# A hybrid decoder layer on one core: the pooling map folded into the output weight, weight parts loaded by another queue, and three edits of order

## The chip, the cores and the metric

The kernel runs on one core of a Trainium2 chip. The metric is the device time of one execution in microseconds (us), as the median of several runs.

## What is computed

One decoder layer over 2048 tokens of width 1024, in fp32. The parts that matter here:

```python
z = rmsnorm(h, g_attn_norm) @ w_in          # q (512), k (128), v (128), u (512)
a = sliding_window_sink_attention(q, k, v, sinks, rel_bias)   # window 128, blocks of 128
# u in 4 groups of 128 channels; group g: trailing mean over 2/4/8/16 tokens, minus the token
pooled = stack((cs - lag) / cnt - u)                          # (S, 4, 128)
m = einsum('bsgc,gcd->bsgd', pooled, w_pool) * pool_scale
h = h + concatenate([a, m]) @ w_out
h = h + (silu(hn @ w_gate) * (hn @ w_up)) @ w_down            # hn = rmsnorm(h, g_ffn_norm)
h = h + sigmoid(rmsnorm(h, g_ple_norm) @ w_ple_gate) * (p @ w_ple_proj)
```

The map of the pooled values, the scale and the lower half of w_out are linear and follow each other: group g of m times its rows of w_out equals pooled_g times (w_pool_g · diag(pool_scale_g) · w_out rows of g).

## The kernel before

**Numbers in two parts.** Every operand of a matmul is split into a high part (an ACT copy that rounds to fp32r, at 1042 for weights) and a low part (DVE's difference, at 1554), and a product is three matmuls: high·high, low·high, high·low. So each panel of weights (128 x 1024, 512 KB) is loaded into raw, split, and used by 24 matmuls of 512 columns.

**Stages.** Tokens go in four tiles of 512. For each tile t there is a z section (10 panels, 20 halves of 12 matmuls: the projections to q, k, v, u) and an output section (8 panels, 16 halves). The order is z0, z1, o0, z2, o1, z3, o2, o3. The attention of a tile is cut into 19 steps that are hosted between halves of later sections (table `HOST`): tile 0 densely in z1, tile 1 in o0 and z2, tile 2 in o1 and z3, tile 3 in o2 and o3. A step's work is spread over all engines: logits, transposes and attention products on TensorE; softmax input, reciprocal, low parts and sums on DVE; exponentials, scaling and copies on ACT; pooling sums and the sinks on GpSimd. After that come, for each half of the tokens, the feed-forward section (seven products by Strassen-like sums), the down projection, and two gate sections (`ple_section`), the first of which is mixed with the norm of the second pair of tiles.

**The pooled values.** GpSimd builds window sums (`sum_level`), DVE forms the mean minus the token (`pool_mean`), ACT and GpSimd split it (`pooled_hi`, `pool_rest`). Then `pool_y` on TensorE maps it with w_pool (2484 to 2486), ACT scales and rounds the result (`pool_y_hi`, 1148) and DVE takes the low part (`pool_y_rest`, 1772), back into the tile's mix buffers. That is done 16 times, at the halves in `POOL_Z`, `POOL_O2` and `POOL_O3`; output sections and, for tile 3, attention products wait for the low part (`y_lo`).

**Queues.** The order of each engine is written out by hand, in program order, with semaphores. SP issues x, raw panels, bias, h, the feed-forward inputs and their stores. Weights of panels 10 to 27 are split once, stored in two parts (`w_split`), and for panels 28 to 71 the parts are fetched again by GpSimd (`load_parts`, 858) into three slots. A pair waits for `panel_used >= i - 2`, that is until the panel three places earlier has been used. In an output section t < 2, eight chunks of x of tile t+2 pass through four stage slots (`load_chunk`, 553): chunk k is scaled by ACT at half 2+k (`CHUNK_AT`) and squared in the half behind it; chunks 4 to 7 reuse the slots. The staging of k and q of the next tile (1087, 1096) is on ACT's list at half 9, and its first logits at half 11 (2392).

**Start.** ACT issues three gains and waits for all (48), then scales x (1056), splits the first panel, and issues eight constants. **Gate.** In the first section of a pair (2677 and on), TensorE turns the added squares (`turn_squares`, 2351) behind the first pair of chunks and the reciprocal roots (2357) behind the second; ACT's four late squares (1049) and GpSimd's sums (824) come just ahead.

The wait for a weight panel differs by its place, which is what the edits of queue touch:

```python
def panel_ready(i):
    if has_parts(i):
        pe.wait_ge(parts_landed[parts_slot(i)], 32 * ((i - SPLIT_END) // SLOTS_W + 1))
    else:
        pe.wait_ge(lo_done, split_of(i) + 1)
```

## Time and profile before

| | |
|---|---|
| median of 3 runs | 2050.03 us |
| lowest and highest | 2048.8 and 2052.91 us |
| the profiled execution | 2053.4 us, span 2051.5 us |
| mean granted clock of TensorE | 0.998 |
| DMA | 292.09 MB, mean 142 GB/s |

PE is TensorE's matmuls, PEld its weight loads (they overlap PE), DVE VectorE, ACT ScalarE, POOL GpSimd, SP the sync engine; a q behind a name is the engine's sequencer. "Idle before it" names what ended an engine's wait; "issue" is time in which it waited for nothing that the profile shows. The granted clock is a share of 2.4 GHz: 0.5 is 1.2 GHz. A landing is counted from the issue. Matmuls overlap at their ends, so that their distance, not their duration, is what one costs.

### The profile page before, as it was taken

What the parts mean: (1) busy time and instruction counts of PE and PEld (TensorE: products, weight loads), DVE (VectorE), ACT (ScalarE), POOL (GpSimd) and SP (SyncE); (2) the same over time, 40 slices, a digit from 0 to 9 for tenths busy, and PEclk for the clock granted to TensorE, in tenths of its full rate; (3) what the DMA queues carried; (4) which work ended last, traced back from release to release, by engine and by line L of the source; (5) the groups of instructions that cost most, each with busy time, mean ns of one, the idle gap of its engine ahead of it and who ended that gap; (6) DMA issues with size and microseconds to landing.
All of it is one profiled execution on the core that took longest, in us unless ns stands there. A gap on an engine that the chain in (4) does not pass through costs nothing.

```text
span 2051.5 us, 26122 instructions
## 1 busy us (share of the span) xinstructions
PE 2011.2 (98%) x9546; PEld 1663.4 (81%) x9546; DVE 1372.9 (67%) x1920; ACT 899.7 (44%) x1460; POOL 406.5 (20%) x508
## 2 busy tenths in 40 slices
PE   8999999999999999999999999999999999999998
PEld 6887878877788888888888878788888888888877
DVE  4696674767696665655888765966566566987663
ACT  4575754657433333333333543533333333334542
POOL 4454644645410000000000220000000000001310
PEclk9999999999999999999999999999999999999999
DMA  7757566364934223225825128432322328352143
GB/s 193 201 180 245 188 236 219 130 236 131 347 127 130 81 72 103 72 72 171 307 62 165 36 72 223 143 119 67 96 85 72 100 79 292 130 159 78 42 134 103
DMA packets 197387, 292.09 MB, mean 142 GB/s; under 512 B 16139, under 2 KB 118452, under 8 KB 195980
## 3 DMA queue, kind: packets, MB, share of 16 engines
q1 hardware_dynamic: 172672, 212.97, 34.1%
q0 software_dynamic: 22176, 76.96, 10.8%
q8 instruction: 76, 1.25, 0.3%
q10 hardware_dynamic: 2412, 0.50, 0.1%
q14 instruction: 51, 0.42, 0.1%
HBM read 223.25 MB, written 67.51 MB: 142 GB/s over the span
## 4 chain that ended last, share of the span: by engine, by line
PE 84%; DVE 6%; DMA 3%; issue 3%; ACT 2%; POOL 1%; SPq 0%; ACTq 0%; DVEq 0%; POOLq 0%
PE bank L2623 13%; PE bank L2627 13%; PE bank L2625 13%; PE bank L2660 7%; PE bank L2661 7%; PE bank L2662 7%; PE bank L2323 4%; PE bank L2325 4%; PE bank L2324 4%; PE bank L2299 2%; PE bank L2301 2%; PE bank L2300 2%; DMA w_parts<-w_split 1%; PE bank L2392 1%; DVE w_lo L1554 1%
## 5 line engine op out<-in xcount | busy, mean ns | idle before, releaser
L2623 PE MATMUL bank<-a_hi,ring_hi 128*128 128x512 f32 x1232 | 479.7, 389 | 1.0 <-DVE ring_lo L1917 0.7
L2627 PE MATMUL bank<-a_hi,ring_lo 128*128 128x512 f32 x1232 | 479.3, 389 | 0.0
L2625 PE MATMUL bank<-a_lo,ring_hi 128*128 128x512 f32 x1232 | 479.3, 389 | 0.0
L2623 PEld LDWEIGHTS bank<-a_hi,ring_hi 128*128 128x128 f32 x1232 | 231.3, 188 | 49.9 <-DVE ring_lo L1917 1.4
L2625 PEld LDWEIGHTS bank<-a_lo,ring_hi 128*128 128x128 f32 x1232 | 231.3, 188 | 48.0
L2627 PEld LDWEIGHTS bank<-a_hi,ring_lo 128*128 128x128 f32 x1232 | 231.3, 188 | 47.8
L2660 PE MATMUL bank<-d_hi 128*128 128x512 f32 x616 | 239.8, 389 | 0.0
L2662 PE MATMUL bank<-d_hi,d_lo 128*128 128x512 f32 x616 | 239.7, 389 | 0.0
L2661 PE MATMUL bank<-d_lo,d_hi 128*128 128x512 f32 x616 | 239.6, 389 | 0.0
L1376 ACT ACTIVATE d_hi<-keep 128x1024 fp32r<-128x1024 f32 x132 | 139.8, 1061 | 201.9 <-PE bank L2662 184.9
L975 POOL DMA_DIRECT2D hidden_T<-hid x88 | 47.6, 541 | 770.4 <-DVE hid L1953 750.7
L2047 DVE TENSOR_TENSOR d_lo<-keep,d_hi 128x1024 fp32r<-128x1024 f32 x132 | 163.9, 1244 | 52.9 <-ACT d_hi L1376 52.8
L1289 ACT ACTIVATE ring_hi<-raws 128x1024 fp32r<-128x1024 f32 x80 | 84.7, 1058 | 218.5 <-PE bank L2627 208.0
L1917 DVE TENSOR_TENSOR ring_lo<-raws,ring_hi 128x1024 fp32r<-128x1024 f32 x80 | 98.7, 1234 | 99.1 <-ACT ring_hi L1289 99.1
L1554 DVE TENSOR_TENSOR w_lo<-raw,w_hi 128x1024 fp32r<-128x1024 f32 x68 | 87.5, 1287 | 100.4 <-ACT w_hi L1042 100.0
L2662 PEld LDWEIGHTS bank<-d_hi,d_lo 128*128 128x128 f32 x616 | 115.6, 188 | 24.2
L2660 PEld LDWEIGHTS bank<-d_hi 128*128 128x128 f32 x616 | 115.6, 188 | 23.9
L2661 PEld LDWEIGHTS bank<-d_lo,d_hi 128*128 128x128 f32 x616 | 115.6, 188 | 23.8
L824 POOL TENSOR_TENSOR acc<-acc,sq 128x512 f32<-128x512 f32 x72 | 110.8, 1539 | 117.8 <-ACT sq L1049 112.8
L1917 DVE TENSOR_TENSOR ring_lo<-t,ring_hi 128x1024 fp32r<-128x1024 f32 x63 | 77.2, 1226 | 66.7 <-ACT ring_hi L1289 66.7
L1042 ACT ACTIVATE w_hi<-raw 128x1024 fp32r<-128x1024 f32 x68 | 71.8, 1055 | 111.5 <-PE bank L2325 63.3
L1289 ACT ACTIVATE ring_hi<-t 128x1024 fp32r<-128x1024 f32 x63 | 66.5, 1056 | 108.2 <-DVE t L1903 108.2
(258 smaller groups left out, 3879.9 us busy)
## 6 DMA issues: line engine op xcount, KB each, us to landing
w_parts<-w_split POOLq DMA_DIRECT2D x88, 512.0 KB, 4.8
hidden_T<-hid POOLq DMA_DIRECT2D x88, 256.0 KB, 2.3
raws<-in_w_gate SPq DMA_DIRECT2D x80, 256.0 KB, 4.7
raws<-in_w_up SPq DMA_DIRECT2D x80, 256.0 KB, 5.1
keep<-hidden_T SPq DMA_DIRECT2D x66, 256.0 KB, 3.8
raw<-in_w_ple_gate SPq DMA_DIRECT2D x64, 256.0 KB, 4.2
keep<-in_w_down SPq DMA_DIRECT2D x44, 256.0 KB, 4.4
other<-hidden_T SPq DMA_DIRECT2D x44, 256.0 KB, 6.8
```

What stands on the lines that cost most here:

```text
L824: nc.gpsimd.tensor_tensor(into[:, :], slots[:, 0, :] if j == 1 else into[:, :], slots[:, j % 2, :], ALU.add).then_inc(acc_done, 1)
L1289: nc.scalar.activation(ring_of(half, m)[0][:, :, :], ring_source(half, m), ACT.Copy).then_inc(ring_hi_done, 1)
L1376: nc.scalar.activation(d_hi[s % SLOTS][:, :, :], down_pair(s)[0], ACT.Copy).then_inc(d_hi_done, 1)
L1554: nc.vector.tensor_tensor(panel_lo(i), panel_raw(i), panel_hi(i).bitcast(F32), ALU.subtract).then_inc(lo_done, 1)
L1917: nc.vector.tensor_tensor(lo[:, :, :], ring_source(half, m), hi[:, :, :].bitcast(F32), ALU.subtract).then_inc(ring_lo_done, 1)
L2047: nc.vector.tensor_tensor(d_lo[s % SLOTS][:, :, :], down_pair(s)[0], d_hi[s % SLOTS][:, :, :].bitcast(F32), ALU.subtract).then_inc(d_lo_do ...
L2623: mm(dst[:, :], wh[:, g, cols], a_hi[o][:, k, :], start=fresh and k == 0, stop=False, skip_group_check=True)
L2625: mm(dst[:, :], wh[:, g, cols], a_lo[o][:, k, :], start=False, stop=False, skip_group_check=True)
L2627: ins = mm(dst[:, :], wl[:, g, cols], a_hi[o][:, k, :], start=False, stop=k == 3, skip_group_check=True)
L2660: mm(dst, wh[:, cols], ah, start=fresh and k == 0, stop=False, skip_group_check=True)
L2661: mm(dst, wh[:, cols], al, start=False, stop=False, skip_group_check=True)
L2662: ins = mm(dst, wl[:, cols], ah, start=False, stop=k == FPAIRS - 1, skip_group_check=True)
```

## The change

Five edits in one:

1. **The pooling map goes into the output weight.** During z0 GpSimd loads the four 128-row groups of w_out's lower half (`load_pooled_rows`); ACT and DVE scale and split them (`pooled_rows_hi`, `pooled_rows_lo`); TensorE multiplies each by w_pool (now loaded transposed), 2 x 3 matmuls per group (`mix_rows`); ACT copies the banks (`copy_mixed`), GpSimd stores them to `w_mixed` (`store_mixed`), and the output panels with pooled rows are read from there. `pool_y`, `pool_y_hi` and `pool_y_rest` are gone, the mix buffers keep the pooled values, and their readers wait for `pool_lo`. Three engines wait at half 4 or 5 of z1 for the stores, SP ahead of the first output panel.
2. **Parts by the sync queue.** `load_parts` moves from GpSimd's list to SP's, between the other transfers; the first four chunks of x and h of tile 1 are issued together at the end of z2 instead of behind it, and the loads of feed-forward inputs in o3 change their order.
3. **The start.** Twelve matmuls on zeros (`WARM`) once the memsets are done; a one-element ACT copy, with which the table is loaded first; ACT waits for one gain instead of three; the other two gains and the eight constants are issued by GpSimd.
4. **The gate's turn.** Turning the squares and the roots comes one pair of chunks later, and so do the sums, scalings and splits that hang on them; the split of the fourth panel stands between the late squares.
5. **u behind attention.** In halves that host a step without fresh logits, DVE copies u behind the step instead of ahead.

```diff
-POOL_Z, POOL_Z_COPY = {14: (0,), 16: (1,), 17: (2,), 18: (3,)}, {15: (0,), 17: (1,), 18: (2,), 19: (3,)}
-POOL_O2, POOL_O2_COPY = {9: (0,), 13: (1,), 15: (2,)}, {9: (0,), 13: (1,), 15: (2,)}
-POOL_O3, POOL_O3_COPY = {0: (3,)}, {0: (3,)}
+POOLED_HI_AT, POOLED_LO_AT = {10: 0, 11: 1, 12: 2, 13: 3}, {11: 0, 12: 1, 13: 2, 14: 3}
+POOLED_AT, POOLED_COPY_AT = {13: 0, 14: 1, 15: 2, 16: 3}, {14: 0, 15: 1, 16: 2, 17: 3}
+POOLED_STORE_AT = {16: (0, 1), 17: (2,), 18: (3,)}
+WARM = 12
...
-                return rows(w_out, 2 * r, 2 * r + 2, cols)
+                return rows(w_mixed[:, :], 2 * r - 4, 2 * r - 2, cols)
...
+            def load_parts(i):
...
+                    sp.wait_ge(panel_used, i - SLOTS_W + 1)
+                sp.wait_ge(parts_stored[kept % 2], 32 * (kept // 2 + 1))
+                for part in range(2):
+                    sp.dma_start(w_parts[parts_slot(i)][:, part, :].bitcast(F32), w_split[kept, part]
+                                   ).then_inc(parts_landed[parts_slot(i)], 16)
...
                     load_z(t + 1, c)
+                    if t == 1 and c == 0:
+                        load_parts(Z_AT[2] + 1)
+                    if t:
+                        load_parts(Z_AT[t + 1] + c + 2)
...
+                    if t == 1 and c == 9:
+                        for k in range(4):
+                            load_chunk(3, k)
+                        for b in range(NB):
+                            load_h(1, b)
...
                     load_out(t, c)
-                    if t == 1 and c == 0:
-                        for k in range(4):
-                            load_chunk(3, k)
-                        for b in range(NB):
-                            load_h(1, b)
+                    if t == 0 and c == 7:
+                        load_parts(Z_AT[2])
+                    if t:
+                        load_parts(OUT_AT[t] + c + 2)
                     if t < 2:
                         for k in {3: (4,), 4: (5, 6), 5: (7,)}.get(c, ()):
                             load_chunk(t + 2, k)
...
+            def pooled_rows_hi(g):
+                if g == 0:
+                    act.wait_ge(consts, CONSTS + 16 * NPOOL)
+                nc.scalar.activation(wo_hi[g][:, :], wo_raw[g][:, :], ACT.Copy,
+                                     scale=scale_sb[:, g:g + 1]).then_inc(wp_hi_done, 1)
...
-                    for j in range(4, KC):
-                        square_late(g + 1, j)
+                    square_late(g + 1, 4)
+                    square_late(g + 1, 5)
+                    split(ple + 3)
+                    square_late(g + 1, 6)
+                    square_late(g + 1, 7)
...
-            act.dma_start(gains[:, 1, :], g_ffn).then_inc(gain_landed, 16)
-            act.dma_start(gains[:, 2, :], g_ple).then_inc(gain_landed, 16)
-            act.wait_ge(gain_landed, 48)
+            act.wait_ge(constants_set, 1)
+            nc.scalar.activation(neg_max[:, 0, 0:1], minus_half[:, :], ACT.Copy)
+            act.wait_ge(gain_landed, 16)
...
-            load_constants()
...
+            def mix_rows(g):
+                pe.wait_ge(wp_lo_done, g + 2)
+                if g == 0:
+                    pe.wait_ge(kvcopied, NB)
+                elif g >= 2:
+                    pe.wait_ge(mixed_copied, 2 * g - 2)
+                for e in range(2):
+                    dst, cols = mixed_bank_of(g, e), slice(e * T, (e + 1) * T)
+                    mm(dst[:, :], wp_hi[:, g, :], wo_hi[g][:, cols], start=True, stop=False)
+                    mm(dst[:, :], wp_hi[:, g, :], wo_lo[g][:, cols], start=False, stop=False)
+                    mm(dst[:, :], wp_lo[:, g, :], wo_hi[g][:, cols], start=False, stop=True
+                       ).then_inc(mixed_bank, 1)
...
-                        pe.wait_ge(y_lo, 4 * t + 2 * r - 2)
+                        pe.wait_ge(pool_lo, 4 * t + 2 * r - 2)
...
-                                if r == 0:
+                                if r == 1:
                                     pe.wait_ge(pp_copied, 8 * g + 4 + 1)
                                     turn_squares(NORM3[g + 1], acc3, bank[BS0[0]])
-                                if r == 1:
+                                if r == 2:
                                     pe.wait_ge(pp_copied, 8 * g + 4 + 2)
                                     turn_rstd(NORM3[g + 1], bank[BS0[1]])
...
+            pe.wait_ge(constants_set, 7)
+            for _ in range(WARM):
+                mm(bank[7][:, :], kT_hi[:, 0:P], vv[:, :, :, :].rearrange("p i j d -> p (i j d)"), start=True, stop=True)
             z_section(0)
```

The sync queue around the second output section, before: the stores of h, the bulk loads, the late four chunks of x (`stage<-in_x`, waiting for squares and norm_lo) and the next store of h.

```order
L558 DMA h_T<-h 128x1024 [waits out_added]
L558 DMA h_T<-h 128x1024 x3
L538 DMA ffn_in_T<-stage 128x1024 [waits norm2_scaled] x4
L553 DMA stage<-in_x 128x512 [waits norm2_stored_odd,norm2_stored_even] x4
L570 DMA h<-in_x 128x1024 [waits h1_stored,norm2_scaled] x4
L553 DMA stage<-in_x 128x512 [waits squares,norm_lo] x4
L558 DMA h_T<-h 128x1024 [waits out_added]
L558 DMA h_T<-h 128x1024 x3
```
And now: between the chunks stand the pairs of weight parts, each waiting for panel_used.

```order
L563 DMA w_parts_96<-w_split 128x1024 [waits parts_stored_odd,panel_used]
L563 DMA w_parts_96<-w_split 128x1024
L579 DMA stage<-in_x 128x512 [waits squares,norm_lo]
L563 DMA w_parts_97<-w_split 128x1024 [waits parts_stored_even,panel_used]
L563 DMA w_parts_97<-w_split 128x1024
L579 DMA stage<-in_x 128x512 [waits squares,norm_lo] x2
L563 DMA w_parts_98<-w_split 128x1024 [waits parts_stored_odd,panel_used]
L563 DMA w_parts_98<-w_split 128x1024
L579 DMA stage<-in_x 128x512 [waits squares,norm_lo]
L563 DMA w_parts_96<-w_split 128x1024 [waits parts_stored_even,panel_used]
L563 DMA w_parts_96<-w_split 128x1024
```
The late chunks 4, 5 and 6, and 7 now stand behind the pairs for panels 43, 44 and 45; before, nothing stood between them.

TensorE at the end of a z section with a hosted tile, before: the three matmuls of the pooling map between halves of the u projection.

```order
L2405 MATMUL bank<-ident,scores 128x128 [waits probsT_copied,k_staged,probs_normalised]
L2405 MATMUL bank<-ident,scores 128x128 x3
L2484 MATMUL bank<-mix_hi,wp_hi 128x512 [waits wp_lo_done,u_copied,pool_lo]
L2485 MATMUL bank<-mix_lo,wp_hi 128x512
L2486 MATMUL bank<-mix_hi,wp_lo 128x512
L2340 MATMUL bank<-wide_hi,w_hi 128x512
L2341 MATMUL bank<-wide_lo,w_hi 128x512
L2342 MATMUL bank<-wide_hi,w_lo 128x512
L2340 MATMUL bank<-wide_hi,w_hi 128x512
L2341 MATMUL bank<-wide_lo,w_hi 128x512
```
And now the same place, where the halves and the attention steps follow each other.

```order
L2447 MATMUL bank<-ident,scores 128x128 [waits probsT_copied,k_staged,probs_normalised]
L2447 MATMUL bank<-ident,scores 128x128 x3
L2382 MATMUL bank<-wide_hi,w_hi 128x512
L2383 MATMUL bank<-wide_lo,w_hi 128x512
L2384 MATMUL bank<-wide_hi,w_lo 128x512
L2382 MATMUL bank<-wide_hi,w_hi 128x512
L2383 MATMUL bank<-wide_lo,w_hi 128x512
L2384 MATMUL bank<-wide_hi,w_lo 128x512
L2382 MATMUL bank<-wide_hi,w_hi 128x512
L2383 MATMUL bank<-wide_lo,w_hi 128x512
L2384 MATMUL bank<-wide_hi,w_lo 128x512
```
The map's matmuls are gone, with their waits for the copy of u and for pool_lo.

ACT in the first gate section, before (`sq` are the late squares, `hn_hi` the split of the normalised values, `raw` the gate's weight panels).

```order
L1406 ACTIVATE proj_first<-bank 128x512 [waits panel_used]
L1049 ACTIVATE sq_188<-h_second 128x512 [waits squares_added,down_added] x4
L1042 ACTIVATE w_hi<-raw_174 128x1024 [waits panel_used,panel_landed_odd]
L1406 ACTIVATE proj_first<-bank 128x512 [waits proj_banks] x3
L1406 ACTIVATE proj_first<-bank 128x512 [waits panel_used]
L1397 ACTIVATE p_hi<-p_raw 128x1024 [waits panel_used,p_landed]
L1042 ACTIVATE w_hi<-raw_174 128x1024 [waits panel_used,panel_landed_even]
L1042 ACTIVATE w_hi<-raw_174 128x1024 [waits panel_used,panel_landed_odd]
L1053 ACTIVATE spread_187<-bank 128x512 [waits rstd_T]
L1421 ACTIVATE hn_hi_second<-stage_179 128x1024 [waits norm3_scaled,down_steps]
L1421 ACTIVATE hn_hi_second<-stage_179 128x1024 [waits norm3_scaled]
```
And now:

```order
L1462 ACTIVATE proj_first<-bank 128x512 [waits panel_used]
L1095 ACTIVATE sq_204<-h_second 128x512 [waits squares_added,down_added] x2
L1088 ACTIVATE w_hi<-raw_190 128x1024 [waits panel_used,panel_landed_odd]
L1095 ACTIVATE sq_204<-h_second 128x512 [waits squares_added,down_added] x2
L1462 ACTIVATE proj_first<-bank 128x512 [waits proj_banks] x3
L1462 ACTIVATE proj_first<-bank 128x512 [waits panel_used]
L1453 ACTIVATE p_hi<-p_raw 128x1024 [waits panel_used,p_landed]
L1088 ACTIVATE w_hi<-raw_190 128x1024 [waits panel_used,panel_landed_even]
L1088 ACTIVATE w_hi<-raw_190 128x1024 [waits panel_used,panel_landed_odd]
L1088 ACTIVATE w_hi<-raw_190 128x1024 [waits panel_used,panel_landed_even]
L1099 ACTIVATE spread_203<-bank 128x512 [waits rstd_T]
```
The fourth panel's split stands between the squares, and the roots' spread one split later.

## Rows read from the trace of the kernel before

**Rows 1.** The page: busy time, and the chain that ended last, by engine.
```profile
span 2051.5 us, 26122 instructions
...
PE 2011.2 (98%) x9546; PEld 1663.4 (81%) x9546; DVE 1372.9 (67%) x1920; ACT 899.7 (44%) x1460; POOL 406.5 (20%) x508
...
PE 84%; DVE 6%; DMA 3%; issue 3%; ACT 2%; POOL 1%; SPq 0%; ACTq 0%; DVEq 0%; POOLq 0%
```

**Rows 2.** TensorE's waits, whole span: us in total, times, longest.
```profile
PE bank L2299 <- DVE w_lo L1554: 10.2, 1, 10.2
...
PE bank L2427 <- issue: 4.2, 3, 1.6
PE bank L2323 <- DVE mix_lo L1772: 3.1, 2, 1.8
PE bank L2351 <- POOL acc L824: 2.6, 2, 1.3
PE bank L2299 <- DMA w_parts<-w_split: 2.1, 1, 2.1
PE bank L2323 <- DMA w_parts<-w_split: 1.9, 2, 1.5
...
PE bank L2323 <- DVE wide_lo L1772: 1.0, 1, 1.0
...
PE bank L2427 <- DVE wide_lo L1772: 0.7, 1, 0.7
```

**Rows 3.** Line L2484: durations in ns, min/median/max, first and last start.
```profile
L2484 PE MATMUL bank<-mix_hi,wp_hi x12: 390/478/481, 135.2 to 431.0; 128*128 128x512 f32 x12
...
L2484 PE MATMUL bank<-wide_hi,wp_hi x4: 392/472/474, 477.4 to 509.6; 128*128 128x512 f32 x4
```

**Rows 4.** The chain in time, first 60 us: start, us, what.
```profile
10.92 0.43 PE bank L2300
...
16.46 0.23 PE bank L2301
```

**Rows 5.** Timeline of ACT, first 80 us: start, us, what, idle before it.
```profile
4.85 1.28 ACT L1056 ACT_TABLE_LOAD   x1 [4.85 <-DMA h<-in_x]
6.47 1.33 ACT L1056 ACTIVATE wide_hi<-h,gains 128x512 fp32r<-128x512 f32 x2 [0.33 <-DMA gains<-in_g_ple_norm]
...
7.71 1.04 ACT L1042 ACTIVATE w_hi<-raw 128x1024 fp32r<-128x1024 f32 x1
...
21.00 1.06 ACT L1042 ACTIVATE w_hi<-raw 128x1024 fp32r<-128x1024 f32 x1 [4.82 <-DMA raw<-in_w_in]
```

**Rows 6.** Stretches: length, busy us by engine, granted clock, DMA.
```profile
1204.00:1212.00 8.00, 6.24 (x23) 4.58 (x22) 5.18 (x4) 4.97 (x8) 2.98 (x4) 0.79 0.29 68
...
366.00:376.00 10.00, 8.07 (x48) 6.25 (x47) 7.03 (x18) 4.96 (x16) 9.16 (x14) 0.83 0.32 106
```

**Rows 7.** Timeline of DVE in the first gate section.
```profile
1205.17 2.22 DVE L1554 TENSOR_TENSOR w_lo<-raw,w_hi 128x1024 fp32r<-128x1024 f32 x1 [4.29 <-ACT w_hi L1042]
...
1222.22 1.23 DVE L1554 TENSOR_TENSOR w_lo<-raw,w_hi 128x1024 fp32r<-128x1024 f32 x1 [1.17 <-ACT w_hi L1042]
```

**Rows 8.** The chain in time, 360 to 373 us.
```profile
368.24 1.93 issue
```

**Rows 9.** Timelines of GpSimd, sync queue, ACT and TensorE, one row each.
```profile
39.60 0.79 POOL L1005 DMA_DIRECT2D band_rows<-band  x1
...
299.80 15.47 SPq L553 DMA_DIRECT2D stage<-in_x  x4
...
326.21 0.28 ACT L1087 ACTIVATE kT_hi<-bank 128x128 fp32r<-128x128 f32 x1 [6.20 <-PE bank L2366]
...
332.01 0.38 PE L2392 MATMUL bank<-kT_hi,qT_hi 64*128 64x256 f32 x2
```

**Rows 10.** DMA issues: lines 858 and, first 60 us, 511; us to landing.
```profile
DMA to landing us min/median/max: 3.7/4.8/12.2
...
raw<-in_w_in SPq DMA_DIRECT2D x22, 256.0 KB, 5.1
```

More of the change, by code:

```diff
@@ L326, in build @@
         last_stored = sem("last_rows_stored")
[L328 removed]
+        CONSTS = 10 * 16
         def ple_at(g):
@@ L938, in z_section @@
                         powers(NORM1[1])
+                    if t == 0:
+                        for g in POOLED_STORE_AT.get(half, ()):
+                            store_mixed(g)
+                    if t == 1 and half == 4:
+                        pool.wait_ge(mixed_stored, 16 * NPOOL)
                     if t >= 2:
@@ L1220, in out_section @@
                         split(OUT_AT[t] + half // 2 + 1)
-                    for g in {2: POOL_O2_COPY, 3: POOL_O3_COPY}.get(t, {}).get(half, ()):
-                        pool_y_hi(3, g)
                     if t < 2 and half in CHUNK_AT:
@@ L1835, in z_section @@
                         normalise2(t - 2, SCALE2_AT[half])
-                    for g in U_COPY_AT[t > 0].get(half, ()):
+                    fresh = any(has_unit(k, 0) and k % 2 == 0 for _, k in hosted_steps("z", t, half))
+                    u_first = fresh or half == 19 or not late
+                    for g in U_COPY_AT[t > 0].get(half, ()) if u_first else ():
                         copy_u(t, g)
@@ L1841, in z_section @@
                         qk_normalise(t, 0)
-                    if t:
-                        for g in POOL_Z_COPY.get(half, ()):
-                            pool_y_rest(t - 1, g)
+                    if t == 0 and half in POOLED_LO_AT:
+                        pooled_rows_lo(POOLED_LO_AT[half])
+                    if t == 1 and half == 5:
+                        dve.wait_ge(mixed_stored, 16 * NPOOL)
                     hosted("z", t, half, Z_AT[t] + half // 2 + 1 if half % 2 == 0 and late else None)
+                    for g in () if u_first else U_COPY_AT[t > 0].get(half, ()):
+                        copy_u(t, g)
             def a_sums(half, i):
@@ L2252, in out_section @@
                     hosted("o", t, half, OUT_AT[t] + half // 2 + 1 if due and late else None)
-                    for g in {2: POOL_O2_COPY, 3: POOL_O3_COPY}.get(t, {}).get(half, ()):
-                        pool_y_rest(3, g)
-            dve.wait_ge(gain_landed, 48)
+            dve.wait_ge(gain_landed, 16)
             norm_lo(0, h[:, 0, :])
@@ L2546, in z_section @@
                         turn_rstd(NORM1[t], bank[3])
-                    if t:
-                        for g in POOL_Z.get(half, ()):
-                            pool_y(t - 1, g)
             def out_section(t):
@@ L2574, in out_section @@
                               behind_first=put_off("o", t, half), before=free)
-                    for g in {2: POOL_O2, 3: POOL_O3}.get(t, {}).get(half, ()):
-                        pool_y(3, g)
                     if t < 2 and half == SUM1_AT:
```

173 lines of the change are left out of this document (82 added, 91 removed).

## Prediction

> **What bounds the kernel now.** I read the page first, then the waits of TensorE, the chain of waits, and the timeline of the stretches that the change touches. The page shows TensorE busy for 98% of the span, and the chain that ended last lies on it for 84% [rows 1]. So what counts is TensorE's own work and the moments at which it stands still. The waits list the latter [rows 2]: 10.2 us before the first matmul; 3.1, 1.0 and 0.7 us for the low part of the pooled map, which DVE writes at line 1772; 2.6 us for the added squares in the gate section; 2.1 and 1.9 us for weight parts that had not landed; 4.2 us that the profile gives to no one before three attention products. A matmul of 512 columns costs 0.23 us where it follows others, and 0.43 us as long as the granted clock stands at its half level [rows 4]. Feed-forward and down sections show no wait worth a term, and the change does not touch their matmuls.
>
> The profiled execution took 2053.4 us (span 2051.5), 3.4 above the median of 2050.0. I sum against the execution and take the difference over to the median. A change under 0.2%, about 4 us, could not be told from none.
>
> **The pooling map moves into the weight: -5.5.** Gone are 16 calls of three matmuls, 12 calls on mix_hi and 4 on wide_hi [rows 3]: 48 x 0.227 = 10.9 us of TensorE. New are 4 x 2 x 3 = 24 matmuls of 512 columns in the first tile's projection, 5.4 us. Ends: 5 and 7, since small waits sit at the changes of operand.
>
> **The wait for the mapped values: -4.8.** The output projection and two attention products waited 3.1 + 1.0 + 0.7 us for line 1772 [rows 2]. They now need only the pooled values, which GpSimd finishes steps earlier (the second pair of order rows). Ends: 0, if other late work of DVE takes the place, and 5.5, because the wait itself plus the start-up after it costs more than the idle time shows.
>
> **ACT and DVE get lighter: -2.** Each loses 16 operations of about 0.7 us in the busiest stretches, and the copy of u now stands behind the attention step. The 4.2 us of late attention products [rows 2] hang on the chain of DVE and ACT there. TensorE arrives sooner as well, since its 0.7 us per call is gone, so I take half. Ends 0 and 4.2.
>
> **Parts by the sync queue: -3.5.** The 44 pairs of weight parts were issued by GpSimd in its own order, behind powers and sums; they landed after 3.7 to 12.2 us, 4.8 in the middle [rows 10]. Twice TensorE ran dry, for 2.1 and 1.5 us, in places where the pair was issued together with the store of h or the loads of the feed-forward inputs, and a third time for 0.4 [rows 2]. On the sync queue the pair stands ahead of those. Ends 0 and 4.5. The Trainium skill, DMA: Bandwidth & Descriptors (Issuing engines are not separate DMA queues), says that transfers run on the same 16 engines whoever issues them, and that another issuer saves only the sequencer's time. By that rule the term is 0 except for the order of issue.
>
> **The same queue now holds back x: +3.** This is the wait that the change adds (first pair of order rows). In the second output section the eighth chunk of x stands behind the pair for panel 45, which waits until panel 42 is used, that is for the end of half 9. Before, the four late chunks were issued between 299.80 and 315.3 with no such condition [rows 9]. On ACT the scaling of this chunk, and a square, precede the staging of k and q for the next tile (lines 1087 and 1096), which started at 326.21, right behind TensorE's transposes. The logits started at 332.01 [rows 9], so there are 5.8 us between. A pair issued at such a place lands after 4.8 us in the middle, 3.7 at best [rows 10], and the chunk, half the size of one part, follows it on the same queue; I take 4.6 for it; ACT then needs 2.3 us and DVE about 1.5: 8.4, so TensorE waits some 2.5 us. Ends 0 and 5. Where it idled for 1.93 us at 368.24, the granted clock over the ten us around it was 0.83 [rows 6, 8], which is some 3.4 us at 1.2 GHz. That can happen here too: 1.7 us more, at even odds. I take 3 in all.
>
> **Rows of the output weight: +1.5.** GpSimd fetches 4 x 512 KB right after the powers in the first section, ahead of the band's second copy, which was issued at 39.60 [rows 9] and may come 2 us earlier now. ACT waits for all four ahead of the split of the eighth panel. Pairs of this size landed after 4.8 us, in crowded places after 12.2 [rows 10]; four, beside panels and x, take some 8 to 13 us from about 37, so until 45 to 50. TensorE wants that panel at about 51, and ACT and DVE need 5 us more for it and what stands ahead. The 8 new copies and 4 roundings on ACT are some 9 us, of DVE 5, in a stretch in which both are idle half the time, so the work itself costs nothing; without that cover it would be up to 9. Ends 0 and 5.
>
> **The head: -1.5.** The first matmul starts at 10.2 [rows 2]. Before it, on ACT: the table load from 4.85, wide_hi at 6.47 when the third gain had landed, w_hi at 7.71 [rows 5]; then w_lo. Without the two gains and with the table loaded before, ACT starts at 4.85, but w_hi needs the panel, whose second half is issued at about 2 and takes 5.1 us in the middle [rows 10]. So the start itself moves by 0.2 or so, at best by 0.6. Then 15 matmuls ran at 0.43 us instead of 0.23 (from 10.2 to 16.46 [rows 4]), 3.0 us. Twelve matmuls on zeros, about 5.1 us at the half level, run from 2 to 7; then the engine rests almost 3 us. Whether the clock is up at 10 is open: after 1.93 us of rest it fell once [rows 6, 8]. I take -1.3 for it; ends 0 and -3.5. Ten constants move from ACT to GpSimd. The third panel, issued while ACT issued eight of them, landed so late that ACT waited 4.82 us for it and started its w_hi at 21.00 [rows 5]. TensorE did not starve there, but a warm start would have made it starve: this is the cover that the warm start needs. GpSimd's first other duty is the sum of squares; ACT's third square waits for it, and a few us of lateness there meet no one.
>
> The Trainium skill, TensorE: Matmul & The Clock Gate (HAM clock gate), states that half rate is the default and sustained activity releases it. The rise after the first matmuls agrees; that a short burst followed by rest holds the clock, no row here shows.
>
> **The gate's turn: -5.** In the two mixed sections TensorE waited 1.3 us each for acc (2.6 in all) [rows 2], and about 0.5 us each for w_lo, which took 2.22 us instead of 1.23 beside GpSimd's sums [rows 7]. In the first of them the granted clock over 8 us was 0.79 [rows 6]: 3.4 us at half level, 1.7 us lost. Now the turn of the squares comes one pair of chunks later, and the panel's split stands between the squares (third pair of order rows). 2.6 + 0.9 + 1.7 = 5.2, less 0.2, because normalising and its two parts now come together just ahead of the second half's panels. Ends 3 and 7.
>
> **Sum:** -5.5 - 4.8 - 2 - 3.5 + 3 + 1.5 - 1.5 - 5 = -17.8. For the execution 2035.6, for the median 2032.2; I say 2032.
>
> **The rivals.** (a) Late transfers at full price: chunk of x 5 + 1.7 and rows 5, in place of 4.5, makes +7.2, so 2039. For it: both stand ahead of staging or splitting on ACT in order. Against: both had time to spare before. Chance 0.2. (b) DVE is the next bound: the terms of 4.8 and 2 come to nothing because attention in the later tiles already ends on DVE and GpSimd holding each other up (as at 368.24 [rows 8]): 2039. Chance 0.13. (c) The head, the parts and the lighter engines pay at their far ends, 2.0 + 1 + 2.2 more: 2027. Chance 0.12. (d) By the rule on issuers: the parts land no earlier and the term of -3.5 is 0: 2036, inside the forecast's own spread; chance 0.1 of its own. The page is DMA: Bandwidth & Descriptors of the Trainium skill. (e) Slower: the sync queue takes its entries in order, and the pairs now stand behind stores that wait for DVE's scaling and for finished sums. A pair is issued about 11 us (two panels of 24 matmuls) before its use and lands after 4.8, so it decides from 6 us of delay at such an entry. There are some 12 such entries in the tiles 3 and 4 and the last section; at 2 us each it is +24, so 2056. Against: the stores follow their producers within one or two halves. Chance 0.03. (f) The warm-up does nothing, and the head costs the same: 2033.5, inside the forecast.
>
> **How the numbers follow.** The forecast with (d) and (f) holds 0.52 (0.42 and 0.1), its own range 2027 to 2037. (a), (b), (c) and (e) hold the rest. The range 2024 to 2042 leaves out (e), the tail of (c) and the joint case of (a) and (b), in all under 0.2. Faster by over 4 us: all but (e) and mishaps: 0.95. Within: 0.02. Slower: 0.03.
>
> **What would show it.** In the new profile: L1772's successors absent from TensorE's waits; no wait for w_parts over 1 us; no wait for acc at the gate and a clock of 1.00 after it; the clock's level at the first real matmul, and whether the third panel's w_hi follows its landing by 16; a wait of 2 to 3 us before the logits of the second output section with ACT waiting for stage<-in_x; ACT's wait for the fetched rows near 45 us and whether TensorE stands still at 51. The prediction is wrong if the waits of the attention stretches grow by what the pooling map gave back, or if GpSimd's ten constants reach the band's matmul (near 30 us) too late.

## The result and the profile after

The changed kernel is slower: 2062.53 us as the median of 8 runs (2057.32 to 2066.98), against 2051.90 for the kernel before (8 runs, 2048.8 to 2054.97). The ratio is 1.0046 with a 95% interval of 1.0034 to 1.0058, so 7 to 12 us lost, where 2032 was forecast. The profiled execution took 2059.2 us (span 2057.4), 3.3 less than the median; the trace therefore explains 5.9 of the some 9.5 us.

The page of the changed kernel, its busy times and the clock, which answer to [rows 1]:

```profile
span 2057.4 us, 26075 instructions
...
PE 2014.2 (98%) x9534; PEld 1664.1 (81%) x9534; DVE 1367.4 (66%) x1908; ACT 899.0 (44%) x1457; POOL 376.9 (18%) x438
...
PEclk9999998999999999999999999999999999999999
```

DVE and ACT did less, but one slice of the clock is down. TensorE's waits, which answer to [rows 2] (in total, times, longest):

```profile
PE bank L2447 <- issue: 5.8, 5, 1.9
PE bank L2341 <- DVE w_lo L1595: 4.9, 3, 2.7
PE bank L2365 <- DVE h L1825: 4.8, 2, 2.5
PE bank L2434 <- DVE qT_lo L1701: 4.1, 1, 4.1
PE bank L2467 <- issue: 3.7, 4, 1.7
PE bank L2365 <- DMA w_parts<-w_split: 3.2, 1, 3.2
...
PE bank L2393 <- POOL acc L859: 1.8, 1, 1.8
PE bank L2651 <- DVE h_last L1825: 1.2, 1, 1.2
```

The waits for the mapped values (mix_lo, wide_lo) and for acc at the gates are gone, as forecast; the 1.8 us for acc that is left stands at the start of the feed-forward section (at 578 us), as does the wait for h_last. In their place stand three in one stretch, from 300 to 350 us: for `h`, which is the bank that DVE has to empty in an output section, for the low part of q, and one of 3.2 us for a pair, where the kernel before waited 0.4. The two kernels there, 50 us each, before and then changed (after the stretch and its length: busy us of PE, PEld, DVE, ACT, POOL with their instructions, granted clock, DMA share, GB/s):

```profile
300.00:350.00 50.00, 49.56 (x244) 40.30 (x243) 23.56 (x51) 14.60 (x35) 24.41 (x33) 1.00 0.68 222
```

```profile
300.00:350.00 50.00, 37.89 (x152) 29.86 (x151) 13.89 (x29) 11.58 (x23) 12.29 (x10) 0.88 0.59 213
```

TensorE stood still for a quarter of it, with a lower clock, and DVE and ACT did less too: nobody was busy, all waited for data.

To place the rest I lined up the start of the same matmul in both traces. The table shows how far the changed kernel is behind (+) at a few of them:

| place | before | changed | behind | step |
|---|---|---|---|---|
| first u panel of z0 | 47.82 | 48.92 | +1.1 | +1.1 start |
| last of them | 68.11 | 76.43 | +8.3 | +7.2: 24 new matmuls 5.4, waits and their ends 1.8 |
| second panel of o0 | 170.68 | 172.42 | +1.7 | -6.6 |
| fourth half of o1 | 306.86 | 304.21 | -2.7 | -4.4 |
| sixth half of o1 | 312.30 | 314.66 | +2.4 | +5.0 |
| last half of o1 | 343.14 | 359.17 | +16.0 | +13.7 |
| last half of o3 | 555.19 | 561.24 | +6.1 | -10.0 |
| first half behind feed-forward and down | 1188.55 | 1200.29 | +11.7 | +5.7 |
| behind the gate's turn, 1 | 1211.96 | 1219.44 | +7.5 | -4.3 |
| behind the gate's turn, 2 | 1955.22 | 1960.59 | +5.4 | -2.1, of it -2.6 at the turn |
| last half | 2042.73 | 2048.80 | +6.1 | +0.7 |

Three steps, +5.0, +13.7 and +5.7, make 24.4 us. Without them the changed kernel would have been 18 us faster than the kernel before. The sync queue around the second output section of the changed kernel (start, time from the first to the last issue of the row, what):

```profile
288.70 0.80 SPq L563 DMA_DIRECT2D w_parts<-w_split  x2
289.54 0.43 SPq L548 DMA_DIRECT2D ffn_in_T<-stage  x1
295.74 1.76 SPq L579 DMA_DIRECT2D stage<-in_x  x4
297.59 2.37 SPq L596 DMA_DIRECT2D h<-in_x  x4
300.05 18.32 SPq L563 DMA_DIRECT2D w_parts<-w_split  x8
318.46 0.38 SPq L579 DMA_DIRECT2D stage<-in_x  x1
323.01 0.80 SPq L563 DMA_DIRECT2D w_parts<-w_split  x2
323.90 0.86 SPq L579 DMA_DIRECT2D stage<-in_x  x2
335.38 0.80 SPq L563 DMA_DIRECT2D w_parts<-w_split  x2
336.28 0.38 SPq L579 DMA_DIRECT2D stage<-in_x  x1
```

The fifth chunk of x went out at 318.46 and the eighth at 336.28; before, all four were issued between 299.80 and 315.3 [rows 9]. What follows a late chunk is in the chain of the changed kernel:

```profile
323.01 0.32 SPq L563
323.38 0.42 SPq L563
323.90 4.73 DMA stage<-in_x
328.65 0.73 ACT wide_hi L1102
...
330.07 0.69 DVE h L1825
330.81 0.79 PE bank L2365
...
335.38 0.33 SPq L563
335.76 0.42 SPq L563
336.28 4.46 DMA stage<-in_x
340.76 0.73 ACT wide_hi L1102
...
342.19 1.29 DVE kT_hi L1682
...
344.70 0.70 DVE qT_lo L1701
345.44 1.65 PE bank L2434 x12
347.09 0.72 PE bank L2365
347.82 0.43 PE bank L2366
```

It is a ring. A pair waits until TensorE has used a panel; the chunk stands behind the pair; ACT scales it, and DVE takes its low part; and behind that, in DVE's program order, stands the emptying of the bank that TensorE needs for the next panel. So a late chunk makes the next panel late, this the next pair, and this the next chunk. After each wait the matmuls run at 0.43 us, the clock's lower level.

### The profile page after: what moved, and what is told of

The parts are those of the page before. It is cut to its first block, busy times and chain, and to the rows that moved or that the text cites. A ratio compares the mean times of both kernels' runs of the same rounds, so it can differ in the third digit from the quotient of the medians.

```text
span 2057.4 us, 26075 instructions
## 1 busy us (share of the span) xinstructions
PE 2014.2 (98%) x9534; PEld 1664.1 (81%) x9534; DVE 1367.4 (66%) x1908; ACT 899.0 (44%) x1457; POOL 376.9 (18%) x438
## 4 chain that ended last, share of the span: by engine, by line
PE 88%; DMA 4%; DVE 3%; issue 2%; ACT 2%; SPq 1%; POOL 0%; ACTq 0%; DVEq 0%; POOLq 0%
PE bank L2651 13%; PE bank L2653 13%; PE bank L2655 13%; PE bank L2688 7%; PE bank L2689 7%; PE bank L2690 7%; PE bank L2365 5%; PE bank L2367 5%; PE bank L2366 5%; PE bank L2341 2%; PE bank L2343 2%; PE bank L2342 2%; PE bank L2434 1%; PE bank L2447 1%; DMA raw<-in_w_ple_gate 1%
```

## The experiments

All times are medians; the kernel before ran beside each group of kernels, with medians of 2053.25 to 2053.91. A ratio is that of a kernel to it. The medians of the kernel before alone lie up to 2 us apart (2051.90 with the result, 2053.91 in one group), so that for small differences between kernels the places in the traces count for more. Rows of the form "behind" are again taken from the same matmul in two traces.

**Chunks ahead of the pairs (x1_chunks).**

```diff
-                        for k in {3: (4,), 4: (5, 6), 5: (7,)}.get(c, ()):
+                        for k in ({2: (4, 5), 3: (6, 7)} if t == 1 else {3: (4,), 4: (5, 6), 5: (7,)}).get(c, ()):
```

> The changed kernel, with one edit: in the second output section the sync queue issues chunks 4 and 5 of x behind the third pair of weight parts, 6 and 7 behind the fourth, ahead of the pairs that stood before them. Theory A (the queue holds x back: a chunk waits behind a pair whose slot is not yet free, ACT and DVE stand behind the chunk, TensorE behind both): TensorE's waits of 2.3, 2.5 and 4.1 us between 325 and 346 go, and with them the half clock behind them; about 12 to 14 us, so about 2049. Rival B (ACT and DVE are late in that stretch for their own work, u behind attention and the folded map): under 3 us, so 2060 or more. Rival C (the pairs now land late instead, behind the chunks): the waits turn into waits for w_parts, 3 to 6 us remain, about 2054.

Measured: 2047.62 us, ratio 0.9974 (0.9964 to 0.9985), so 15 us less than the changed kernel. In its trace the 13.7 us are gone to the last hundredth: it is 7.99 behind at the eighth half of o1 and 7.99 at the last. Theory A holds for this term. The wait for the pair stayed and was larger (5.0 us):

```profile
PE bank L2365 <- DMA w_parts<-w_split: 5.0, 1, 5.0
```

**The loads of h behind a pair (s2_chunks_h)**, on top of the last.

```diff
                         for k in range(4):
                             load_chunk(3, k)
-                        for b in range(NB):
-                            load_h(1, b)
...
                     if t:
                         load_parts(OUT_AT[t] + c + 2)
+                    if t == 1 and c == 1:
+                        for b in range(NB):
+                            load_h(1, b)
```

> The kernel of x1_chunks, with one more edit: the four loads of h (1 MB) go behind the pair of the second output panel instead of ahead of the first pair. In x1_chunks TensorE waited 5.0 us for w_parts at 315, with the clock at half behind it, some 7.7 us in all. Theory A (the pair stands in the queue behind the bulk of x and h and shares the engines with it): the wait shrinks to 1.5 us or less and the clock stays up, 5 to 6 us gained, about 2042. Rival B (the pair is held back by the queue's wait for the last store of the normalised values to land, ahead of the bulk): 3 us or more remain, about 2046. The kernel before had 0.6 there.

The four loads are 2 MB together, not the 1 MB that the expectation names. Measured: 2044.37 us, ratio 0.9956 (0.9942 to 0.9969); 3.2 us less than x1_chunks by the medians, with intervals that overlap. In the trace the wait for w_parts is gone altogether, and a smaller one for the bank has come at 322:

```profile
PE bank L2366 <- DVE h L1826: 2.1, 2, 1.6
```

The three halves at 305 to 312 are 7.7 us better than in x1_chunks, this wait takes 1.9 back; the 5.8 that are left are what theory A said, though the medians show less. The store of the normalised values still had to land before the chunks; that it cost nothing here speaks against rival B.

**Weight parts by GpSimd again (p1_parts_pool).** `load_parts` and its calls go back to GpSimd's list, and `load_a(0, 2)` behind `load_a(0, 1)` and `load_a(0, 3)`:

```diff
+                    if t >= 2 and half % 2 == 0:
+                        load_parts(Z_AT[t] + half // 2 + 2)
```

> The changed kernel with its second part undone: the weight parts are issued by GpSimd again at its old places, and the loads of the feed-forward inputs in their old order; folded map, start, gate's turn and u behind attention stay. Theory A (all that was lost after 300 us was lost in the sync queue's order): the 18.7 us lost between 304 and 352 and the 5.7 lost at the start of the feed-forward section go, waits for w_parts of 3 to 4 us come back: about 2042 (2038 to 2046). Rival B (other parts of the change cause the losses): 2055 or more. Under A the four other parts together are worth 8 to 12 us against the kernel before.

Measured: 2049.49 us, ratio 0.9980 (0.9972 to 0.9989). Faster than before by 4, but 7 short of what theory A said. The 13.7 and the 5.7 are gone in the trace; a wait for a pair in o1 is not. It is 4.2 us, but for another pair: that of panel 39, at the third half, where the changed kernel waited for that of panel 40, at the fifth. The kernel before had 0.4 at the third half. There GpSimd issued the pair at 295.13 us, here at 300.09, 5.0 later and behind its powers, while TensorE was only 2.0 later (at 299 us), having been 4.8 behind at 235. So the folded map has let TensorE catch up with a pair that GpSimd issues late. Another part of the 7 lies in the first section, which is 3.5 us worse in this trace than in the changed kernel's (11.8 against 8.3 behind at the last u panel).

**Stores of tile 2's values ahead of two pairs (n1_stores).**

```diff
-                if c == 4:
-                    store_n2(2, 0)
-                    store_n2(2, 1)
-                if c == 5:
-                    store_n2(2, 2)
-                    store_n2(2, 3)
+                if c == 3:
+                    for b in range(NB):
+                        store_n2(2, b)
+                if c == 5:
```

> The changed kernel, with one edit: in the last output section the four stores of tile 2's normalised values are issued behind the pair for panel 69, ahead of the two pairs that they stood behind. Theory A (these stores are held back by pairs that wait for a slot, the first feed-forward weights wait for the stores to land, and so TensorE waits at the start of the feed-forward section): the 5.7 us go, with the half clock at 580; about 2057. Rival C (too much is to be moved there, whatever the order): under 1.5 us, so 2061 or more.

Measured: 2060.49 us, ratio 1.0037 (1.0024 to 1.0049); 2 us less than the changed kernel, whose interval overlaps. The trace decides: the waits at the feed-forward's start are gone (-0.5 where it was +5.7), but a wait of 2.1 us for a pair came at 557, with the clock at half level behind it, +4.0 us more in the last output section. Both theories are half right. The wait at the start was due to the order of the stores, as A said; and with that order alone the loss only moved, as C said: the loads of the feed-forward inputs, 1 MB each, had gone out late as well, from 526 to 534 us where three of them had left from 511 to 513 before (TensorE was 7 to 9 us behind here), so that loads, stores and pairs met in 20 us. That it is so "whatever the order", all2 below refutes: it moves these loads ahead too, and both losses are gone.

**Constants behind the first sum of squares (c1_consts).**

```diff
                             add_squares(NORM1[0], j, sq, acc)
+                            if j == 1:
+                                load_constants()
...
-            load_constants()
             z_section(0)
```

> The changed kernel, with one edit: GpSimd issues the ten constants and gains behind its first sum of squares, at about 10 us, instead of ahead of it from 1.9 us on. Theory A (ten small-row loads fill the queues ahead of the second panel's second half and the third pair of x): the second panel lands near 11.5 instead of 15.95, TensorE's wait of 1.4 us at 18.4 goes; the third panel then queues behind the constants as in the kernel before and the wait of 0.9 at 25.0 stays: 1.4 to 1.7 us gained, about 2061. Rival D (the second panel is late because its own issue and the engines' total are what bounds): no change. If instead everything after it is on time, 2.6 us: 2060.

Measured: 2057.85 us, ratio 1.0030 (1.0019 to 1.0040), some 3 us less than the changed kernel by the ratios, 1.5 of them at the start in the trace (0.4 ahead of the kernel before at 47.8 instead of 1.1 behind). Both waits for w_lo at 18 and 25 us are gone, so both belonged to the early constants; theory A had the second one stay. In the five runs with them issued first, the first u panel came 1.0, 1.0, 1.1, 1.3 and 3.2 us behind, so this loss also differs from run to run.

**The gate's turn alone, on the kernel before (g1_gate_only).** The fourth part of the change, word for word; one of its places:

```diff
-                                if r == 0:
+                                if r == 1:
                                     pe.wait_ge(pp_copied, 8 * g + 4 + 1)
                                     turn_squares(NORM3[g + 1], acc3, bank[BS0[0]])
```

> The kernel before, with the fourth part of the change alone (the gate's turn). Theory A (the squares, their sums and the panel's low part no longer meet; each section loses its wait, the first its throttled stretch too): 4.3 and 2.6 us less in the two sections, 0.6 back ahead of the second half's panels, 6.2 in all: about 2047.1, ratio 0.997. Rival B (the gain in the changed kernel came from the different start of these sections): 3 us or less, 2050 or more.

Measured: 2047.79 us, ratio 0.9971 (0.9960 to 0.9982): 5.7 us less. In the trace the two turns give 4.26 and 2.57 us, to the hundredth what they give in the changed kernel. Theory A holds.

**All repairs together (all2).** x1_chunks, s2_chunks_h, c1_consts, n1_stores, and in the last output section the loads of the feed-forward inputs earlier:

```diff
                 if c == 0:
                     store_h1(2)
-                if c == 1:
                     load_a(0, 0)
-                    load_a(0, 2)
-                if c == 2:
                     load_a(0, 1)
                     load_a(0, 3)
+                if c == 2:
+                    load_a(0, 2)
```

> The changed kernel with four repairs: the chunks of x ahead (x1_chunks), the loads of h behind a pair (s2_chunks_h), the constants behind the first sum (c1_consts), and in the last output section the loads of the feed-forward inputs ahead of the pair of the second panel and the stores of tile 2's values behind the fourth. Theory A (all losses of the changed kernel come from what stands behind what in a queue): 2034 (2030 to 2039), with no wait over 2 us between 300 and 350 and under 1 us at the feed-forward start. Rival C (what is moved ahead makes the pairs late in turn, the sum of the transfers is what bounds these stretches): 2041 or more.

Measured: 2037.29 us, ratio 0.9921 (0.9908 to 0.9934). The feed-forward start costs 0.15 instead of 5.7. Theory A, in the upper part of its range.

**Rows of w_out issued ahead of the band's store and the powers (all2_rows).**

```diff
+                            load_pooled_rows()
                             store_band()
                             powers(NORM1[0])
-                            load_pooled_rows()
```

> The kernel of all2, with one more edit: GpSimd issues the four loads of w_out's rows ahead of the band's store and the powers in the first section instead of behind them (about 3 us earlier). Theory A (TensorE's waits of 0.5 and 0.9 us at 55 and 58 end on the last row landing at 52.9): 1 to 1.7 us less than all2. Rival (the rows then collide with panels and x at 35 to 45 us and the wait moves): no gain, or up to 1 us lost.

Measured: 2035.57 us, ratio 0.9916 (0.9903 to 0.9929). The medians of the two lie 1.7 apart with intervals that overlap; in the trace both waits at 55 to 58 us are gone and the second u panel starts 2.5 us earlier. No other kernel here is faster beyond the noise; the one without the matmuls on zeros, below, is its equal. TensorE's waits in it:

```profile
PE bank L2446 <- issue: 5.7, 4, 1.9
PE bank L2466 <- issue: 3.8, 4, 1.7
PE bank L2340 <- DVE w_lo L1594: 3.5, 1, 3.5
PE bank L2466 <- DVE probsT_lo L1717: 2.1, 3, 1.0
PE bank L2742 <- POOL u L1061: 2.0, 1, 2.0
PE bank L2364 <- DMA w_parts<-w_split: 1.1, 1, 1.1
PE bank L2364 <- DVE h L1824: 1.0, 1, 1.0
```

What is left is, for the most part, the starts of the transposes and attention products (L2446, L2466), of which only the fifth part of the change touches what stands ahead.

**All repairs, but weight parts by GpSimd (p2_pool_repaired).** With the pairs gone from the sync queue, the late chunks of x, the stores and the feed-forward inputs go back to their old order; the loads of h wait until TensorE has used panel 38, o1's first.

> The kernel of all2_rows with the weight parts issued by GpSimd instead of the sync queue (chunks of x need no repair there; constants, rows and the loads of h as in all2_rows; feed-forward inputs in their old order). Theory A (issued by the sync queue, a pair is no longer held up by GpSimd's powers and sums, and once the queue's order is right the forecast term of 3.5 us is real): 3 to 5 us slower than all2_rows (2035.6), 2039 to 2041, with waits for w_parts at about 225, 305 and 530. Rival D (the transfers share the same engines, so the issuer changes nothing): within 1.5 us of all2_rows.

Measured: 2044.34 us, ratio 0.9954 (0.9940 to 0.9967), 8.8 us slower than all2_rows. In the traces, whose ends lie 13.0 apart, 8.7 us arise at one place, the fifth half of o1, where TensorE waits 6.4 us for a pair. GpSimd's timeline there:

```profile
294.02 1.26 POOL L853 TENSOR_TENSOR qk_sq<-qkv 128x640 f32<-128x640 f32 x1
...
295.67 1.98 POOL L880 TENSOR_TENSOR qrs<-qms,minus_half 128x10 f32<-128x10 f32 x1
...
298.61 2.33 POOL L880 TENSOR_TENSOR qrs<-qms,minus_half 128x10 f32<-128x10 f32 x1
300.89 2.20 POOL L869 DMA_DIRECT2D w_parts<-w_split  x4
```

And the sync queue of all2_rows at the same work:

```profile
294.59 4.82 SPq L563 DMA_DIRECT2D w_parts<-w_split  x4
```

There the pair went out at 294.6 and landed at 301.4; GpSimd came to it at 300.9, behind its powers, and it landed at 310.3, beside the loads of h and two more pairs. So 6.3 of the 8.9 us are the later issue, and 2.6 a longer way in that company. Theory A, with twice the size that it expected, though not by the issuer alone: the last output section, where the feed-forward inputs stand in their old order, shows 1.8 us in the trace.

**Without the matmuls on zeros, and with 26 (w0_no_warm, w26_warm)**, both on all2_rows.

```diff
-WARM = 12
+WARM = 0
```

```diff
-WARM = 12
+WARM = 26
```

> The kernel of all2_rows without its twelve matmuls on zeros. In that kernel's trace the clock is up from 5.5 to 8.9 us and at half level again when the first real matmul starts at 10.16, until 15.7. Theory A (a warm-up that ends 3.5 us ahead of the work is lost): no difference, within 1 us of all2_rows (2035.6). Rival (a part of it lasts: the clock rises earlier after the first real matmul than it would cold, as in the kernel before, where it took 6.2 us): 0.5 to 1.5 us slower.

> The kernel of all2_rows with 26 matmuls on zeros instead of twelve, so that they end near 9.6 us, right ahead of the first real one. Theory A (the clock holds if the engine doesn't rest): the 12 or 13 matmuls at 0.43 us run at 0.23, 2.5 us less: about 2033; panels two and three, landed as before, may take back up to 1 us. Rival (the start is bound by the panels that land, not by the clock): the gain of 2.5 turns into waits for w_lo before 25 us, under 1 us is left.

Measured: 2035.09 us (ratio 0.9913, 0.9899 to 0.9927) and 2036.84 us (0.9917, 0.9904 to 0.9931), against 2035.57 with twelve. TensorE in the 6 us from 10 on, first with twelve, then with 26:

```profile
10.00:16.00 6.00, 5.84 (x14) 4.65 (x15) 3.74 (x5) 4.77 (x7) 6.00 (x9) 0.52 1.05 265
```

```profile
10.00:16.00 6.00, 6.00 (x28) 4.99 (x27) 4.35 (x6) 4.36 (x7) 6.00 (x9) 1.00 0.98 261
```

In the kernel with twelve they brought the clock up at 5.5 us; their last ended at 6.6, the clock fell at 8.9, and the real ones, from 10.16, ran at half level until 15.7. Without any, the real ones started at 9.56 and the clock rose at 14.0. With 26 it held, and twice as many matmuls ran (the first few of them still on zeros). Yet at 47.8 us only 0.5 was left of that: the zeros themselves held the first real matmul up until 10.66 (9.56 without any), and TensorE then waited 1.1 us for the panel at 47. Theory A for the twelve, the rival for the 26.

**u ahead of attention again (u1_u_first)**, on all2_rows.

```diff
-                    u_first = fresh or half == 19 or not late
+                    u_first = True
```

> The kernel of all2_rows with the fifth part of the change undone: DVE copies u ahead of the attention step again. Theory A (the step's DVE work decides when the transposes and attention products of the z sections can start, and they still wait 1.9, 1.7 and 1.3 us): 0.7 us more in each of some 3 to 5 such places, 2 to 4 us slower, 2038 to 2039. Rival B (DVE and GpSimd hold each other up there whatever stands first): within 1 us.

Measured: 2040.27 us, ratio 0.9933 (0.9918 to 0.9948). 4.7 us more by the medians, with intervals that just overlap. The trace has 3.6 of them in z1, where TensorE waits 2.4 us for an attention product at 156 and then runs at the clock's lower level; so theory A, and the clearest part of it in one place. The profiled execution was the slowest of the six (2043.51), and its trace has other losses beside this one.

**The folded map alone, on the kernel before (m1_map_only).** The first part of the change, with nothing of the others: `mix_rows` and what belongs to it; parts by GpSimd, ACT's constants and gains, the early turn, u first.

> The kernel before with the first part of the change alone: the pooling map in the output weight; parts by GpSimd, start, gate's turn and u ahead of attention as before. By the terms forecast for it (5.5 and 4.8 and part of 2 gained, 1.5 lost at the rows): 9 to 10 us less, about 2044. Theory A (the map's matmuls and waits are worth all of that, and the sequel pays): 0.79 us for each of the 16 calls, 12.6 in all, against 5.4 for the 24 new matmuls, 4 to 5 for waits, less 1.5 at the rows and 3 to 4 for the wait for w_parts at 305 to 310, which comes because TensorE now gets there earlier than the pair lands: 6 to 8 us less, about 2046. Rival (the gain is taken up by DVE's copy of u ahead of attention, as u1_u_first suggests): 2 to 4 less, 2050.

Measured: 2056.39 us, ratio 1.0017 (1.0007 to 1.0026): slower than the kernel before by some 3 us, where the forecast's terms and both theories said faster. TensorE's waits in it:

```profile
PE bank L2361 <- DMA w_parts<-w_split: 7.1, 3, 5.1
PE bank L2463 <- issue: 6.9, 4, 2.4
...
PE bank L2337 <- DMA w_parts<-w_split: 2.6, 1, 2.6
```

The first section costs 7.6 us more (5.4 for the new matmuls, 1.6 of waits at the rows, the rest behind them). z1 gives only 2.9 back instead of 6.6, since the attention product at 160 us waits 2.4. And the pairs, issued by GpSimd as before, cost 9.7 us of waiting instead of 4.0 [rows 2]: 2.6 at 227 and 5.1 at 311. The matmuls and the wait for the mapped values are gone here too, but what they give back turns into other waits. That u behind attention and earlier pairs are what keeps it in the whole kernel is read from these places; no run adds them to this kernel one by one.

## Why the prediction was wrong

It was right in which terms of the gain exist and, in most, in their size. The step that failed is the term "the same queue now holds back x", forecast at +3 and measured at +18.7. Beside it the sum had nothing for the last output section (+5.7), and the start came out as a loss.

- **The map in the weight** (-5.5): -7.2. A call of three matmuls cost 0.79 us, not 0.68; the steps at single calls in z3 and o2 are all 0.78 to 0.80. The new ones cost the 5.4 forecast.
- **The wait for the mapped values** (-4.8): -5.1, from four steps of 1.52, 1.57, 0.73 and 1.26. Right, wait and start-up together.
- **ACT and DVE lighter** (-2): what the other terms leave of the sum is about -3, 1.9 of it in z1. u1_u_first and m1_map_only, where the 16 operations are dropped as well and an attention product in z1 waits 2.4 us, point to the copy of u behind attention as what carries it.
- **Parts by the sync queue** (-3.5): as the change does it, a loss. With the queue's order repaired it gives 8.8 us (p2_pool_repaired), more than the far end of 4.5. The rule of the Trainium skill, DMA: Bandwidth & Descriptors (Issuing engines are not separate DMA queues), has another issuer save only the sequencer's time; the forecast's rival (d) made nothing of that. The traces show what it left out: GpSimd came to the pair of panel 40 only behind its powers, 6.3 us later than the sync queue, and TensorE waited 6.4.
- **The queue holds back x** (+3): this is the step that failed. It measured +13.7, and with the 5.0 of the late pair +18.7. The forecast looked at one entry, the eighth chunk ahead of the logits, and priced one wait there (4.1 us instead of 2.5). It left out the three chunks before it, and that DVE empties TensorE's bank behind each of them; so it did not see the ring. It also named the pair for its issue but not what stood ahead of it: chunks and h, 3 MB, waiting themselves for a store to land. x1_chunks takes the 13.7 away by order alone, and s2_chunks_h the wait for the pair.
- **The same in the last output section**: not in the sum. Loads and stores for the feed-forward part went out some 5 to 11 us later relative to TensorE (but for one load, which did not), +5.7. Rival (e) came closest: it had pairs late behind stores, 24 us in twelve places. That the three places measured make 24.4 is luck, since they are the other way round, chunks and stores late behind pairs. It was given 0.03 because the stores follow their producers in time. What matters is the other side: how long the entry ahead of them blocks, and a pair blocks for a whole panel by design.
- **Rows of w_out** (+1.5): +1.8; all2_rows takes it away.
- **The start** (-1.5): +1.1. In this trace 8 matmuls ran at the lower level rather than 15, which gave some 1.2 us, but that is not shown to be the warm-up's doing: g1_gate_only and m1_map_only have none, and their clock rose 3.0 and 4.2 us after the first matmul, against 6.2 in the kernel before and 3.5 here. The start itself came 0.45 earlier. The second and third panel then cost 2.8 us, 2.3 of them as waits. The forecast asked whether GpSimd would be late with the constants, not what the constants would hold up.
- **The gate's turn** (-5): -5.7, which is 6.8 at the two turns less 1.1 given back behind them, and 5.7 by the medians measured alone.

The forecast's sum, 17.8 us, is what the repaired kernel gains: all2_rows has 0.9916, 17 us. That is chance in part, since there parts by the sync queue give more and the start less than was forecast.

## To carry to other kernels

Before an entry moves to an in-order queue, list what it waits for and for how long by design, then everything that stands behind it up to the next such entry, and follow each of those to whoever waits for it; if the end of that line is what the entry itself waits for, it is a ring and costs on every turn. Neither side is safe by rule: the chunks of x had to go ahead of the entries that wait for a slot (x1_chunks), the loads of h behind one (s2_chunks_h), and stores moved ahead made a pair late (n1_stores). What decides is who is waited for first. Take a part's worth from a run of that part alone only with care: the folded map loses 3 us alone and is what brings TensorE ahead of its transfers in the whole.

## What the chip showed

Ten small loads (constants and gains, rows of 4 to 1536 bytes), issued by GpSimd from 1.87 to 7.66 us, held up the sync queue's large ones: the second half of the second panel, issued at 3.86, landed at 15.95; with the constants issued from 11.26 us on (c1_consts), it was issued at the same time and landed at 11.93. The third panel, issued at 10.67 beside the eight constants of ACT, landed at 20.97 in the kernel before; in c1_consts, issued at 10.84, at 15.68.

In all2_rows the clock fell back 2.3 us after the last of the twelve matmuls on zeros. Behind that rest it was up again 5.6 us after the first real matmul, against 4.4 in w0_no_warm. One pair of traces proves little here, but all of them say the same: the clock rose 3.0 to 6.2 us after the first real matmul in the four kernels without a warm-up, and 2.9 to 5.8 us after it in the ten with twelve. The Trainium skill, TensorE: Matmul & The Clock Gate (HAM clock gate), has half rate as the default that sustained activity lifts; these traces agree, and the short burst was worth nothing.
